# Half of the attention probabilities transposed by VectorE and placed by DMAs through DRAM

## The reference, cut to what matters

```python
def one_block(qblk):
    s = jnp.einsum('bqhd,bkhd->bhqk', qblk, k).astype(F32) * scale
    p = jax.nn.softmax(s, axis=-1).astype(v.dtype)
    return jnp.einsum('bhqk,bkhd->bqhd', p, v)
```

## Time and profile before

| | |
|---|---|
| runs | 1644.56, 1645.06, 1647.28 us |
| profiled execution | span 1645.5 us, first to last instruction; its own time is not listed apart |
| TensorE busy | 1633.9 us, 99% of the span |
| VectorE, ScalarE, GpSimd busy | 1043.6, 571.0, 1026.5 us |
| attention heads | from 113 to 317 us |
| granted TensorE clock | mean 0.997 of full speed |
| DMA | 220.61 MB, mean 134 GB/s |

### The profile page before, as it was taken

One profiled execution on the slowest core, in us unless ns is written; L12 is line 12 of the kernel. 1 busy time (PEld: TensorE's weight loads), 2 busy tenths in 40 slices (PEclk: granted clock), 3 DMA queues, 4 the chain that ended last, 5 costly groups with the idle time before them and its releaser, 6 DMA issues.

```text
span 1645.5 us, 24018 instructions
## 1 busy us (share of the span) xinstructions
PE 1633.9 (99%) x8950; PEld 1364.2 (83%) x8950; DVE 1043.6 (63%) x1537; ACT 571.0 (35%) x1017; POOL 1026.5 (62%) x656
## 2 busy tenths in 40 slices
PE   9999999999999999999999999999999999999998
PEld 7887778798888888889887798888888898888887
DVE  3567777677877865635487566655558359746173
ACT  3467777633233232203344243222222121123111
POOL 3455766656666766575579456666676645567663
PEclk9999999999999999999999999999999999999999
DMA  9234335232269863435322233344434253223332
GB/s 371 87 90 129 111 106 165 79 93 96 89 211 320 298 225 103 141 137 172 120 90 65 77 99 102 125 156 140 153 106 143 97 214 120 65 84 103 91 101 90
DMA packets 59095, 220.61 MB, mean 134 GB/s; under 512 B 6849, under 2 KB 9153, under 8 KB 55682
## 3 DMA queue, kind: packets, MB, share of 16 engines
q1 hardware_dynamic: 53826, 204.96, 38.2%
q10 hardware_dynamic: 5184, 14.49, 2.3%
HBM read 201.07 MB, written 14.16 MB: 131 GB/s over the span
## 4 chain that ended last, share of the span: by engine, by line
PE 95%; DVE 4%; ACT 0%; issue 0%; DMA 0%; DVEq 0%; SPq 0%; ACTq 0%
PE PS L2444 28%; PE PS L2446 28%; PE PS L2445 28%; PE PS L2821 3%; PE PS L2783 2%; PE PS L1012 1%; PE PS L2430 1%; PE PS L1785 1%; PE PS L2595 1%; DVE SC L3572 0%; DVE WA L1990 0%; PE PS L1791 0%; DVE MR L3522 0%; PE PS L2720 0%; PE PS L2721 0%
## 5 line engine op out<-in xcount | busy, mean ns | idle before, releaser
L2354 POOL TENSOR_TENSOR WL<-RAW,WH 128x1024 fp32r<-128x1024 f32 (+3 forms) x211 | 542.8, 2572 | 17.6
L2444 PE MATMUL PS<-HH,WH 128*128 128x512 f32 (+1 forms) x1340 | 507.5, 379 | 0.0
L2446 PE MATMUL PS<-HH,WL 128*128 128x512 f32 (+1 forms) x1340 | 502.9, 375 | 0.0
L2445 PE MATMUL PS<-HL,WH 128*128 128x512 f32 (+1 forms) x1340 | 502.9, 375 | 0.0
L2351 POOL TENSOR_SCALAR WH<-RAW 128x1024 fp32r<-128x1024 f32 (+3 forms) x211 | 239.4, 1134 | 287.8 <-PE PS L2446 276.5
L2444 PEld LDWEIGHTS PS<-HH,WH 128*128 128x128 f32 x1340 | 252.2, 188 | 50.7 <-issue 6.2
L2446 PEld LDWEIGHTS PS<-HH,WL 128*128 128x128 f32 x1340 | 252.2, 188 | 45.9
L2445 PEld LDWEIGHTS PS<-HL,WH 128*128 128x128 f32 x1340 | 252.3, 188 | 43.9
L2379 POOL TENSOR_SCALAR PR<-PR,SC 128x768 f32<-128x768 f32 x47 | 107.3, 2292 | 66.7 <-DVE SC L3579 66.3
L2444 PE MATMUL PS<-HIDH,WH 128*128 128x512 f32 (+1 forms) x396 | 145.3, 367 | 0.0
L2445 PE MATMUL PS<-HIDL,WH 128*128 128x512 f32 (+1 forms) x396 | 144.8, 366 | 0.0
(11 more groups left out here) (532 smaller groups left out, 2894.6 us busy)
## 6 DMA issues: line engine op xcount, KB each, us to landing
RAW<-in_wup SPq DMA_DIRECT2D x88, 512.0 KB, 3.6
MRF<-in_modw SPq DMA_DIRECT2D x52, 512.0 KB, 4.8
RAW<-in_wdn SPq DMA_DIRECT2D x32, 704.0 KB, 4.1
MR<-in_modw SPq DMA_DIRECT2D x28, 512.0 KB, 3.6
RAW<-in_whin SPq DMA_DIRECT2D x24, 512.0 KB, 3.5
MK<-in_modk SPq DMA_DIRECT2D x8, 1024.0 KB, 10.9
RAW<-in_wo SPq DMA_DIRECT2D x8, 512.0 KB, 4.2
hy_hs<-HST ACTq DMA_DIRECT2D x4, 1024.0 KB, 4.0
```

What stands on the lines that cost most here:

```text
L2354: pool.tensor_tensor(WL[s][:, 0:n], raw[:, 0:n], WH[s][:, 0:n].bitcast(F32), ALU.subtract).then_inc(tile_split, 1)
L2444: pe.matmul(out, wh, xh, start=first, stop=False)
L2445: pe.matmul(out, wh, xl, start=False, stop=False)
L2446: return pe.matmul(out, wl, xh, start=False, stop=last)
```

## The change

Query tiles 0 and 1 of every head (`BLOCKED = 2`) leave TensorE's transposes. ScalarE writes their exponentials with the keys regrouped, so that each 32 x 32 block lies together; VectorE transposes the blocks in place (`block_turn`), one instruction for a tile of 128 x 768; SyncE writes each tile to DRAM (`blocks_out`) and reads them back in eight transfers to the new tile `PB` (`blocks_in`), which sets the blocks of 32 queries at the partitions of their keys. TensorE transposes tiles 2 and 3 only, twelve blocks a head, and `value` reads `PB` for its first half and the halved `PT` for its second. ScalarE scales tiles 2 and 3, GpSimd 0 and 1. `PB` has one buffer. The modulation rows are set otherwise: eight before head 0, two in head 0 and in each odd head, three in heads 13 and 14. SyncE's loop is unrolled. Some semaphores are merged.

```diff
+BLOCKED = 2
+PRE_ROWS = 8
-        PT = r.put("PT", [P, 6, L])
+        PB = r.put("PB", [P, 4, BLOCKED, 6, 32])
+        PT = r.put("PT", [P, 6, P * (4 - BLOCKED)])
+        d_blocks = nc.dram_tensor("pr_blocks", (2, P, BLOCKED, LK), F32).ap()
...
+            def blocks_out(h, qt):
+
+                sp.wait_ge(S["turned"], BLOCKED * h + qt + 1)
+                sp.dma_start(d_blocks[h % 2, :, qt, :], PR[h % 2][:, qt, :]).then_inc(S["blocks_out"], 16)
+
+            def blocks_in(h):
+
+                sp.wait_ge(S["pv"], h + 1)
+                sp.wait_ge(S["blocks_out"], 16 * BLOCKED * (h + 1))
+                for qt in range(BLOCKED):
+                    for m in range(4):
+                        sp.dma_start(PB[:, m, qt, :, :].rearrange("p t j -> p (t j)"),
+                                     d_blocks[h % 2, 32 * m:32 * m + 32, qt, :].rearrange("k (c x) -> c k x", c=4)
+                                     ).then_inc(S["blocks_in"], 16)
...
+            for r in range(PRE_ROWS + 2):
+                mod_load(16 + r)
+                if r == 1:
+                    head_weights(2)
...
+            for h in range(16):
+                if h % 2 and h < 11:
+                    head_weights(h // 2 + 3)
+                elif h == 11 or h == 13:
+                    ring("wo", a["wo"], h // 2 - 5)
+                if h > 12:
+                    for r in range(3 * h - 17, min(3 * h - 14, EARLY)):
+                        mod_load(16 + r)
+                elif h % 2:
+                    mod_load(16 + PRE_ROWS + 1 + h)
+                    mod_load(16 + PRE_ROWS + 2 + h)
...
+                for qt in range(BLOCKED):
+                    blocks_out(h, qt)
+                blocks_in(h)
+            x_again(1)
...
-                for qt in range(3 if h else 2):
+                for qt in range(2):
                     c = (4 * h + qt) % 8
                     pool.wait_ge(S["rcp"], 4 * h + qt + 1)
...
+            def turn(h, n):
+
+                if n == 0:
                     if h == 0:
                         pe.wait_ge(S["kready"], key_hi_at(0) + 2)
+                    else:
+                        pe.wait_ge(S["pt"], 5 * h + 1)
+                if n == 2:
+                    pe.wait_ge(S["pt"], 5 * h + 2)
+                for kt in (2 * n, 2 * n + 1):
+                    for qt in range(BLOCKED, 4):
+                        q = (kt % 2) * 256 + (qt - BLOCKED) * P
+                        m = pe.transpose(PS[:, 6 + n % 2, q:q + P], PR[h % 2][:, qt, kt * P:(kt + 1) * P], IDENT[:, :])
+                m.then_inc(S["s_tr"], 1)
...
+                pe.wait_ge(S["blocks_in"], 16 * 4 * BLOCKED * (h + 1))
                 for kt in range(6):
-                    pe.wait_ge(S["pt"], 7 * h + kt + 2)
-                    for half in range(2):
-                        m = pe.matmul(PS[VH * half:VH * half + VH, out_bank(h), 0:256], V[:, kt, v],
-                                      PT[:, kt, tok(half)], start=kt == 0, stop=kt == 5)
+                    pe.wait_ge(S["pt"], 5 * h + kt // 2 + 2)
+                    pe.matmul(PS[0:VH, out_bank(h), 0:256].rearrange("p (i m j) -> p i m j", i=2, m=4), V[:, kt, v],
+                              PB[:, :, :, kt, :].rearrange("p m i j -> p i m j"), start=kt == 0, stop=kt == 5)
+                    m = pe.matmul(PS[VH:2 * VH, out_bank(h), 0:256], V[:, kt, v], PT[:, kt, :], start=kt == 0, stop=kt == 5)
...
+                out, src = PR[h % 2][:, qt, :], wide(2 * (qt % 2), LK)
+                if qt < BLOCKED:
+                    out, src = out.rearrange("p (c t j) -> p t c j", c=4, t=6), src.rearrange("p (t c j) -> p t c j", t=6, c=4)
...
+            def block_turn(h, qt, i=0, per=0):
+
+                dve.wait_ge(S["pnorm"], i * (2 * per) + (2 * h + qt + 1))
+                dve.transpose(PR[h % 2][:, qt, :], PR[h % 2][:, qt, :]).then_inc(S["turned"], 1)
...
+                if h < 15:
+                    block_turn(h + 1, 0, i, per)
                 if h % 2:
                     row(1)
+                if h in (13, 14):
+                    row(2)
+                if h < 15:
+                    block_turn(h + 1, 1, i, per)
                 out_lo(h, i, per)
...
+            pre_rows(6, 8)
+            for qt in range(BLOCKED):
+                block_turn(0, qt)
+            head(0)
```

More of the change, by code:

```diff
@@ L3123, in head @@
                 turn_copy(h, 0, i, per)
+                if h % 4 == 0 and per:
+                    mod_store(i)
                 for kt in range(1, 6):
-                    turn_copy(h, kt, i, per)
+                    if kt == 1 or kt == 3:
+                        turn_copy(h, (kt + 1) // 2, i, per)
                     if kt == 1 and h % 4 == 3 and h < 12:
@@ L3137, in head @@
                 if h < 15:
+                    normalise(h + 1, i, per, 2)
                     normalise(h + 1, i, per)
@@ L3145, in head @@
                     query_hi(3)
-                if h % 2 and h < 14:
-                    mod_store(2 * h - 2, 4, i, 2 * per)
             rope_hi(0)
@@ L3589, in out_lo, with head @@
                                       ALU.subtract).then_inc(S["olo"], 1)
-            def head(h, rows, i=0, per=0):
+            def block_turn(h, qt, i=0, per=0):
+                dve.wait_ge(S["pnorm"], i * (2 * per) + (2 * h + qt + 1))
+                dve.transpose(PR[h % 2][:, qt, :], PR[h % 2][:, qt, :]).then_inc(S["turned"], 1)
+            def head(h, i=0, per=0):
                 def row(k):
-                    if rows:
-                        if k == 0 and h % 2 == 0 and h:
-                            dve.wait_ge(S["modx"], i * (per // 2) + h // 2)
-                        mod_rows(rows[k], i, 2 * per, MACC[:, rows[k] % 4:rows[k] % 4 + 1], MR, CB[:, :])
+                    if h == 0:
+                        r = PRE_ROWS + k
+                    elif h == 15:
+                        return
+                    elif h > 12:
+                        r = PRE_ROWS + 3 * (h - 13) + 14 + k
+                    elif h % 2:
+                        r = PRE_ROWS + 2 + h - 1 + k
+                    else:
+                        return
+                    if per:
+                        if h == 1 and k == 0:
+                            dve.wait_ge(S["modx"], i + 1)
+                        mod_row(r, MACC[:, r - PRE_ROWS - 2:r - PRE_ROWS - 1], i, per)
+                    else:
+                        mod_row(r, MOD[:, 16 + r:17 + r])
                 late_row = h % 4 == 0 and 0 < h <= 12
```

151 lines of the change are left out of this document (64 added, 87 removed).

## The result

Changed kernel: 1772.45 us median (1770.1 to 1776.38, 4 runs); kernel before, on the same chip: 1646.17 us (1644.56 to 1647.37, 4 runs). The ratio is 1.077, 95% interval 1.0753 to 1.0787: 126 us slower. The forecast was 1745, range 1672 to 1805.

What follows compares the result with a forecast made beforehand. TensorE, busy for 1633.9 of 1645.5 us, was taken as the bound, with its waits for PB added in full: 1645.5 + 86 for later value products + 13 for the clock = 1745 us, range 1672 to 1805.

Steps and rivals of the forecast that it cites:

- V(0): Start of head 0's value products, forecast at 138.6 us against 125.0 before; other numbers in brackets mean other heads.
- the clock: TensorE's granted clock falling after standing still about eleven times: 13 us added, bounds 0 and 37.
- the start: Before head 0's value products: eight rows done about 122, two transposes 1.8, write 2.95, reads 11.8 us.
- the steps into heads 13 and 14: Value products to value products, with the third row load ahead of the write: 23.2 us each.
- Removed, 24.3 us: Ceiling of the gain: 21.1 us from fewer TensorE transposes, 3.2 from rows no longer between two maxima.
- Rival 2: Exchange through DRAM hides once its time falls under about 13.6 us; about 1635 us, chance 0.09.
- OUT: From a head's last score to its blocks landed in DRAM: 11.9 us for odd heads, about 9 for even.
- IN: Eight transfers of a head into PB: 11.8 us, 9.7 moving over four engines and 2.1 issue, travel, receipt.
- Rival 1: Reads spread over sixteen engines, taking 7.0 us: 1684, or 1695 with some falls of the clock; chance 0.21.
- S(h): End of head h's last score, made while head h-1 runs on TensorE.
- The steps: Value products of one odd head to the next: 34.3 us, or 32.9 with one projection.
- Value products read PB in runs of 32: Value products' reading pattern in PB: 0 taken, at most another 1.4 us per head at half rate.

Runs made afterwards that it cites:

- e3: Changed kernel with the exchange through DRAM left out for heads 1 to 15, block transposes kept: 1683.75 us.
- e6: e3 with VectorE's block transposes also left out for heads 1 to 15: 12.5 us faster than e3.
- e1_spread: Changed kernel with each of the eight reads of a head taking 32 source rows outermost instead of 4: 1703.87 us.
- e4_early: e1_spread with both block transposes ahead of the key remainders and of the second and third modulation rows: 1701.53 us.
- e7_tail: e4_early with SyncE's order changed at heads 12 to 15, so no row load or load of X precedes a write of blocks: 1689.07 us.
- e12_busy: Changed kernel with 30 more value-shaped products a head on TensorE before the wait for PB: 86.9 us more.
- e9_noex_scale: e3 with ScalarE's scaling of tile 2 ahead of the last exponential, in some nine heads: 2.7 us less than e3.
- e5: e3 with VectorE taking the next tile's maximum before the reciprocal, three places a head outside the late-row order: 6.4 us more than e3.
- e10_noex_outlo: e3 with VectorE's remainder of the head's output ahead of the next head's block transposes: 17.6 us slower than e3.

## Why the prediction was right, and where its sizes were off

The mechanism held: TensorE loses more by waiting for PB than it saves. Of the 124.1 us between the spans, 20.5 are at V(0), 100.9 between V(0) and V(15), 2.7 behind. The forecast had 13.6, 72.4 and none, and 13 for the clock on top, 25 us less in sum. Some 12 of these are the clock; the start is 7 us later, and the steps into heads 13 and 14 are 9.9 longer (3 of them the clock again).

**Removed, 24.3 us.** TensorE's work fell, by 192 instructions and in four heads without the exchange by 4.3 us of the 5.3 reckoned. But "the ceiling of the gain is 24.3 us, if everything new is hidden" is wrong in its condition: with the exchange gone (e3) the heads take 12.5 us longer than before, with the block transposes gone too (e6) still 2.4. Rival 2's "the wait vanishes when OUT + IN falls under 13.6" was priced by TensorE's work alone. The kernel before had VectorE and ScalarE close behind TensorE, at 75% and 76% of the stage, with the order of their handovers fitted to it; the likely reading is that 1.3 us less a head only uncovered them. It is not shown: e6_noex_noturn still has the rest of the change (one scaling more on ScalarE, the rows in other places, transposed tiles copied two at a time, merged semaphores), and only the place of the scaling was tried.

**IN, 11.8.** Measured 11.2 to 13.1, median 12.5. Four engines were right, and they gave 93 GB/s, 33 ns a piece instead of 38. Moving is thus 8.5 us and the rest, issue, travel and receipt, about 4 instead of 2.1: two errors that nearly cancel. The Trainium skill, "DMA: Bandwidth & Descriptors", section on why a DMA increments by 16, has the rule for the number of engines (the largest up to 16 that divides the slowest dimension); the completion packets agree, 4 to a transfer here and 16 in e1_spread, whose slowest dimension is 32.

**Rival 1, 1684 to 1695.** Its kernel now exists, e1_spread: 1703.87. IN was better than said, 6.0 (median) against 7.0; the start (138.0 against 134), V(12) (315.1 against 306) and the steps into heads 13 and 14 (19.8 and 23.4 against 18.5 each) were worse. The last step was 10.2, as its sum implies. Its first step, to V(1) = 149, doesn't follow from its terms: 155.7 less twice 4.8 is 146. The measured V(1) is 151.1.

**OUT, 11.9.** VectorE's transpose took 0.96 us (0.9 forecast; 958 ns mean, 32 times); the estimate of 1.9 us does not hold here. It was worked out from what the Trainium skill, "VectorE: DVE Perf Modes", section on the three transpose paths, gives for a bf16 tile of 128 x 128, while this one is float32 and 128 x 768. The write was mis-sized: landing 3.9 us median, up to 8.1, against 2.6. It is queued behind weights, rows and QR moves, and these land later too while four engines carry the reads (row loads 7.3 us; in e1_spread 4.6, and the write 2.6). The four engines are not all of it: in e4_early and e7_tail, with sixteen, the write landed in 3.7 and 4.1. OUT as a whole, from S(h) to the first read, was 10.9 and 11.1 us at heads 5 and 9, and 13.8, 13.7 and 13.3 at heads 3, 7 and 11.

**The steps.** V(3) to V(5) 32.9 and V(7) to V(9) 33.6, forecast 32.9; V(1) to V(3) 38.7, V(5) to V(7) 38.7 and V(9) to V(11) 38.3, forecast 34.3. The two that fit do so by luck: from V(3) to S(5) it took 1.7 us more than forecast, mostly since the value products ran at the lower clock, and OUT and IN of head 5 were 1.0 and 0.6 shorter. In the step to V(7) the 1.7 stand as well, but OUT and IN are 1.8 and 1.0 longer instead; what sets heads 3, 7 and 11 apart on SyncE is that QR moves stand beside the loads ahead of the write. The start: rows done at 125.8 (122), then write 2.4 longer and IN 0.8: V(0) 145.5 (138.6). Heads 13 and 14: 26.8 and 29.5 us instead of 23.2; the third row load was named but priced too low, and the megabyte of X ahead of head 14's write was not named. e7_tail moves both out of the way and shows what they cost together: on top of e4_early 17.2 us in these two steps, of which 3.0 come back in the next.

**The clock, 13.** It cost some 25 us (e12_busy and what is said there); the step that failed is "I take 13, as not each will fall for so long". From the first to the last start, value products took 3.8 to 4.7 us in 15 of 16 heads, against 2.4 at full clock. Only head 6, ahead of which TensorE stood still for just 1.75 us, kept the 2.4.

**Value products read PB in runs of 32: 0.** Right: 379 ns by either half in e3.

**Scaling moved: nothing.** In the changed kernel it doesn't show. With the exchange out, TensorE waits 8.1 us for ScalarE's scaling, and another place for it brought 2.7 us at most (e9_noex_scale); no run gave it back to GpSimd.

## What to carry to other kernels

Before work is taken off the busiest engine, read the handovers of the engines next to it: here TensorE had 99% and VectorE and ScalarE 75% in the stage, and removing 8% of TensorE's work gave nothing even with the exchange and the block transposes left out. For a strided transfer look which dimension is outermost, on the side with the smallest one, and count the completion packets: the same bytes in the same number of transfers cost 69 us more when 4 instead of 32 stood there. What is queued ahead of a short transfer that something waits for, on its queue and on its engines, belongs to its latency.

## What the runs showed of the hardware

**VectorE's row waits for GpSimd's subtraction.** A row took 1.18 to 1.25 us at most places, but 1.7 to 4.0 at some. VectorE and GpSimd in e3_noex:

```profile
189.95 2.49 DVE L3548 CUSTOM_DVE_ANT_0 MR<-MR,CB 128x1024 f32<-128x1024 f32 x1
192.37 0.08 DVE L3548 DVE_READ_ACCUMULATOR2_ANT SC<- 128x1 f32 x1
192.37 0.97 DVE L3620 STREAM_TRANSPOSE PR<-PR 128x768 f32<-128x768 f32 x1
```
```profile
188.45 2.91 POOL L2387 TENSOR_TENSOR WL<-RAW,WH 128x1280 fp32r<-128x1280 f32 x1
```

GpSimd ends at 191.36, the row 1.08 later at 192.44. The same sum holds in the changed kernel (198.91 and 199.99), in e6 (190.14 and 191.23) and in e5 (196.33 and 197.40): the row starts its 1.08 us when GpSimd's pass over two SBUF operands ends. The block transpose beside it (189.05, 0.98 us, one operand) was not held. In e5 rows of over 2 us stood at seven heads, against three in e3, which would fit its 6.4 us; but rows of this kind alone decide little, since e6_noex_noturn has them as well and is faster, and e10_noex_outlo has none after 126 us and is slower. No run took this apart. The Trainium skill, "SBUF — State Buffer", section on its two separate sides, says that a VectorE operation with two SBUF inputs and a GpSimd operation that reads SBUF lock each other out of a shared port pair for a whole instruction. The trace agrees for GpSimd's subtraction. It does not for GpSimd's scaling, which reads SBUF too: in the kernel before a row of 1.23 us (200.97) ran beside three scalings that took 6.73 us together (from 197.88), and neither was held.

**Pieces of 768 bytes.** Four engines moved 93 GB/s, sixteen some 225: 33 and 55 ns a piece on each engine, so the rate does not grow in proportion.

**Issue.** The issue of a read of 96 KB took SyncE 544 ns with a dimension of 4 outermost and 432 with one of 32 (medians), and 451 with twice the bytes.
